# Opening of a two-block transformer kernel: modulation blocks at every second pooled tile, four of them placed behind the means

## What is computed

```python
s_c = jax.nn.silu(c)                                   # c: one vector of 1024
mod_x = s_c @ mod_w[i] + mod_b[i]                      # 1024 x 6144
sh1, sc1, g1, sh2, sc2, g2 = jnp.split(mod_x[:, None, :], N_MOD, axis=-1)
hx = x * (1.0 + sc1) + sh1
ox, oc = pool_mixer(hx, hc, pool_w[j], pool_scale[j], not last)
x = layer_norm(ALPHA * x + g1 * ox, ln_g[i, 0], ln_b[i, 0])
x = layer_norm(ALPHA * x + g2 * swiglu(x * (1.0 + sc2) + sh2, ffn_w_in[i], ffn_w_out[i]), ...)
```

## Time and profile before

| | us |
|---|---|
| median of three runs | 2856.98 |
| the three runs | 2854.58, 2856.98, 2862.43 |
| the profiled execution, its own time | 2859.71 |
| its span in the trace | 2858.0 |
| PE busy in the span | 2719.1 (95%) |
| DVE, ACT, POOL busy | 1496.9, 1031.8, 1379.0 |

### The profile page before, as it was taken

The page is one execution under the profiler, slowest core; times in us unless marked ns, Lnnn a source line. Parts: engine busy times, 40 slices in busy tenths (PEclk is TensorE's granted clock), DMA queues, the critical chain, the costliest instruction groups (busy, mean ns, idle before and its releaser), DMA issues.

```text
span 2858.0 us, 39137 instructions
## 1 busy us (share of the span) xinstructions
PE 2719.1 (95%) x14026; PEld 2175.0 (76%) x14026; DVE 1496.9 (52%) x2276; ACT 1031.8 (36%) x1792; POOL 1379.0 (48%) x895
## 2 busy tenths in 40 slices
PE   7999999999988999999997999999989999998998
PEld 2588888888766777777776888888778788886775
DVE  6665445445456555665556563645483022325666
ACT  3642222322253333333332233132442455554332
POOL 0587676676643322212221333433254477776564
PEclk9999999999999999999998999999999999998999
DMA  9211111111121101000110111111222222223333
GB/s 386 95 52 52 44 59 51 48 55 51 45 82 39 38 22 33 33 29 30 36 30 23 52 52 44 52 51 52 89 97 103 103 89 88 81 80 114 109 103 139
DMA packets 67519, 202.25 MB, mean 71 GB/s; under 512 B 17620, under 2 KB 23892, under 8 KB 65256
## 3 DMA queue, kind: packets, MB, share of 16 engines
q1 hardware_dynamic: 46624, 169.46, 17.8%
q10 hardware_dynamic: 20808, 31.61, 3.2%
HBM read 171.61 MB, written 29.44 MB: 70 GB/s over the span
## 4 chain that ended last, share of the span: by engine, by line
PE 87%; DVE 6%; ACT 2%; issue 2%; DMA 1%; POOL 1%; ACTq 0%; DVEq 0%; SPq 0%; POOLq 0%
PE ps L1046 27%; PE ps L1048 26%; PE ps L1047 26%; PE ps L1459 2%; PE ps L1114 1%; PE ps L1470 1%; DVE acc L2944 1%; PE ps L1839 1%; PE ps L1222 1%; PE ps L1189 1%; DMA mod_big<-mod_w 1%; PE ps L1200 0%; PE ps L1507 0%; PE ps L1147 0%; DVE da_al L3161 0%
## 5 line engine op out<-in xcount | busy, mean ns | idle before, releaser
L734 POOL TENSOR_TENSOR slab_hi<-slab_raw,zero 128x1024 fp32r<-128x1024 f32 x103 | 199.6, 1938 | 991.2 <-PE ps L1048 901.9
L1046 PE MATMUL ps<-h_hi,slab_hi 128*128 128x512 f32 x1616 | 645.6, 400 | 12.4 <-POOL h_lo L752 7.0
L1047 PE MATMUL ps<-h_lo,slab_hi 128*128 128x512 f32 x1616 | 634.5, 393 | 0.0
L1048 PE MATMUL ps<-h_hi,slab_lo 128*128 128x512 f32 x1616 | 633.6, 392 | 0.0
L1046 PEld LDWEIGHTS ps<-h_hi,slab_hi 128*128 128x128 f32 x1616 | 305.8, 189 | 89.0 <-issue 12.9
L1048 PEld LDWEIGHTS ps<-h_hi,slab_lo 128*128 128x128 f32 x1616 | 305.6, 189 | 66.6
L1047 PEld LDWEIGHTS ps<-h_lo,slab_hi 128*128 128x128 f32 x1616 | 306.0, 189 | 60.1
L738 POOL TENSOR_TENSOR slab_lo<-slab_raw,slab_hi 128x1024 fp32r<-128x1024 f32 x103 | 252.2, 2449 | 9.7 <-DVE mean L3044 1.7
L2970 DVE SCALAR_TENSOR_TENSOR resid<-ps,mod,resid 128x512 f32<-128x512 f32 x320 | 224.7, 751 | 0.5 <-issue 0.3
L799 POOL TENSOR_TENSOR slab_lo<-slab_raw,slab_hi 128x512 fp32r<-128x512 f32 x124 | 162.1, 1315 | 43.3 <-ACT slab_hi L2070 42.7
L1048 PE MATMUL ps<-t_hi,slab_lo 128*128 128x512 f32 x368 | 143.9, 391 | 0.0
(11 more groups left out here) (459 smaller groups left out, 5924.5 us busy)
## 6 DMA issues: line engine op xcount, KB each, us to landing
slab_raw<-w_in SPq DMA_DIRECT2D x168, 512.0 KB, 3.6
mod_big<-mod_w SPq DMA_DIRECT2D x12, 2048.0 KB, 12.1
slab_raw<-w_c SPq DMA_DIRECT2D x43, 512.0 KB, 4.1
res_scr<-resid ACTq DMA_DIRECT2D x4, 2048.0 KB, 7.2
resid<-res_scr ACTq DMA_DIRECT2D x2, 4096.0 KB, 12.4
gv_scr<-sg_t ACTq DMA_DIRECT2D x4, 2048.0 KB, 7.3
slab_raw<-gv_scr SPq DMA_DIRECT2D x16, 512.0 KB, 3.4
uz_scr<-gu_out SPq DMA_DIRECT2D x16, 512.0 KB, 3.1
```

Source lines behind the costliest of these rows:

```text
L734: pool.tensor_tensor(hi, raw[slot][:], zeros, ALU.add).then_inc(hi_done.sem, 1)
L1046: pe.matmul(dst, w_h, r_h, start=first, stop=False, skip_group_check=True)
L1047: pe.matmul(dst, w_h, r_l, start=False, stop=False, skip_group_check=True)
L1048: return pe.matmul(dst, w_l, r_h, start=False, stop=last, skip_group_check=True)
```

## The change

In the loop over pooled tiles a block and its columns stand at j = 3, 5 and 7 instead of at 2 to 6. Blocks 8 to 11 now lie behind the last means: 8 ahead of the spread of the means, 9 behind it, 10 between squares 3 and 4, 11 behind square 7 as before. ACT's copies of the rows 8, 9 and 10 move with them. SP's and POOL's lists are the same.

```diff
             for j in range(2, KT):
                 pool_tile(j)
                 pool_means(j - 2)
-                if j < 7:
-                    mod_block(j + 3)
-                if j == 4:
-                    pe.wait_ge(mod_col.sem, 4)
-                if j < 7:
-                    mod_columns(j + 2)
+                if j % 2 == 1:
+                    mod_block((j + 7) // 2)
+                    if j == 7:
+                        pe.wait_ge(mod_col.sem, 4)
+                    mod_columns((j + 5) // 2)
             pool_means(KT - 2)
             pool_means(KT - 1)
-            mod_columns(9)
+            mod_block(8)
+            mod_columns(7)
             for e in range(2):
                 spread_mean(0, e)
+            mod_block(9)
+            mod_columns(8)
+            for k in range(KT // 2):
+                square_part(0, 0, k)
             mod_block(10)
-            for k in range(KT):
+            mod_columns(9)
+            for k in range(KT // 2, KT):
                 square_part(0, 0, k)
             mod_block(11)
             spread_rstd(0, 0)
...
-            for n in range(4, 10):
+            for n in range(4, 8):
                 mod_read(n)
             act.activation(warm[:], eps[:], ACT.Sqrt)
...
             for e in range(2):
                 mean_out(0, e)
-            for n in range(5):
+            mod_read(8)
+            for n in range(2):
+                square_centred(0, n)
+            mod_read(9)
+            for n in range(2, 6):
                 square_centred(0, n)
             mod_read(10)
-            for n in range(5, KT):
+            for n in range(6, KT):
                 square_centred(0, n)
```

## The result

| us | before | changed |
|---|---|---|
| median (22 runs each) | 2861.68 | 2866.84 |
| lowest and highest | 2853.81, 2863.78 | 2858.14, 2870.17 |
| span of the profiled execution | 2858.0 | 2868.0 |

The changed kernel takes 1.0018 times as long as the one before, 95% interval 1.0012 to 1.0025: 5.2 us more, where +5.0 was forecast. The absolute forecast of 2862 stood on the median of three runs of before, 2857.0. Over 22 runs that median is 2861.7, and the changed kernel's 2866.8 lies that much higher too: as an absolute time it is 0.2 us inside the upper end of the forecast range (2855 to 2867) and where rival 3 stood. What the forecast had right is the difference.

The account below looks back on a forecast made before the run. PE was taken to bound the kernel, full from 140 to 200 us, so opening shifts reach the end. Slabs +3.0 and clock +2.0 us on the median 2857 gave 2862 us, range 2855 to 2867.

Parts of the forecast that it names:

- rival 3: Wait for square 11 passes 5.5 us, loads 10 and 11 each slow: 8.5 us slower, 2866 us or more; chance 0.14.
- Pooling loop, 4.0 us earlier: Turns 2, 4 and 6 lose block and columns, so the means are spread at 84.0 instead of 88.02 us.
- Given back behind the means, root 1 us earlier (0.3 to 4): Between means and reciprocal root an extra block and columns, up to 3.7 us, leave the root 1 us earlier.
- Slabs 10.3 us later: Slab loads queue behind loads 10 and 11, so the first slab lands at 94.0 instead of 83.70 us.
- POOL free at 102.7, sum of square 11 3.6 us later: POOL's idle 6.71 us is eaten up; square 11 starts at 102.7 instead of 99.08 us, and PE's sum waits.
- The list behind it is full, so all shifts: PE's list is full from 102.20 to 112.34 us, so everything to the last opening wait comes 3.0 us later.
- The clock, 2.0 us (0 to 4): PE's gap of 4.1 to 5 us before square 11's sum drops the clock to half, costing 2.0 us.
- Rival 1: Slabs late in the opening but the clock holds: only the 3.0 us, 2860 us; chance 0.20.
- Rival 2: Slabs load beside loads 10 and 11, so aren't late: 1 to 4 us gained, 2853 to 2856 us; chance 0.18.
- Rival 4: Clock gaps later in the kernel fall differently, 2 to 4 us each in either direction; no chance of its own given.

Follow-up runs that it names:

- e1: Changed kernel with both slab loads issued ahead of load 10 instead of behind load 11; ratio to the kernel before 0.9992 (0.9984 to 1.0001).
- e8: Changed kernel with both slab loads ahead of load 10, the same edit as e1 timed again; ratio to the kernel before 0.9991 (0.9981 to 1.0000).
- e2: Kernel before with both slab loads issued ahead of load 10; ratio to the kernel before 0.9992 (0.9983 to 1.0002).
- e3: Kernel before with its two slab loads held back until block 10 has been used; ratio to the kernel before 1.0018 (1.0009 to 1.0026).
- e4: Changed kernel with 20 matmuls without use filling PE's gap ahead of its sum of square 11; ratio to the kernel before 1.0006 (0.9997 to 1.0015).
- e7: Changed kernel, unchanged, profiled a second time; the execution took 2867.10 us.
- e9: Changed kernel with both slab loads issued between loads 10 and 11; ratio to the kernel before 1.0008 (0.9999 to 1.0018).
- e5: Kernel before, unchanged, profiled a second time; the execution took 2862.10 us.
- e6: Kernel before, unchanged, profiled a third time; the execution took 2860.27 us.

## Why the prediction was right, step by step

- **Pooling loop, 4.0 us earlier.** Right: the spread stands at 84.08, forecast 84.0, and 3.8 us earlier in the same view.
- **Given back behind the means, root 1 us earlier (0.3 to 4).** Right: the root is spread at 95.66, in before at 96.97. DVE idles 2.73 us for `mod_columns(9)`, which stand behind block 10. e1 and e8 show the net gain of this line alone: 1.3 to 1.5 us at the last wait, against a profile of before at full clock. Against e2, whose slabs are as early and whose clock fell, it is 2.9 to 3.2 us, 1.6 of them from the sum of square 11 to that of square 15 (13.74 us against 12.14 and 12.16).
- **Slabs 10.3 us later.** Right in cause, short by 0.7: load 11 and the slabs went out at 83.3 and 83.67, the first slab was used at 94.74 (forecast 94.0). e3 shows that late slabs alone make the whole loss, and e1 that without them there is none.
- **POOL free at 102.7, sum of square 11 3.6 us later.** Short by 1.0: POOL was free at 103.66 and the sum came 4.57 us later. 0.7 of it is the slab. The rest is mostly the second `slab_lo`, 2.69 us where 2.41 had been taken from a stretch in which DVE was less busy (2.94 us of the 4 from 88, against 3.71 of the 4 from 100).
- **The list behind it is full, so all shifts.** Right. Of the 4.57 us, 0.67 go in PE's own idle time (11.49 us from sum to sum at full clock, 12.16 before), so the slabs cost 3.9 us where 3.0 was forecast.
- **The clock, 2.0 us (0 to 4).** Right mechanism, term mis-sized: 3.5 and 2.5 us in the two profiles, against a run of the same list at full clock (e4), and 3.1 us in e3. The gap was 6.35 us (6.34 in e7) where 4.1 to 5 was forecast, for two reasons: the square was 1 us later, and PE had finished squares 8 to 10 at 98.4 already.
- **What the sum left out** evens this out: before, too, loses some 1.5 us of clock in the same place, in two of its three profiles, and the profile on which the sum rested had not. How often it does so in executions that were not profiled is not known. 3.9 and 3.5 make +7.4 at the opening, which is right for that one pair of profiles; +5.2 is what the medians say. Two terms too small and one left out partly cancel, so that the +5.0 fell so close to it is luck; the mechanism is not.
- **Rivals.** Rival 1 (clock holds) is refuted by the clock at 0.50. Rival 2 (slabs not late) is refuted, and e1 built it. Rival 3 came nearer in the first pair of profiles than the forecast did: the gap passed its 5.5 us, and the clock stood at 0.50 from 104 to 112 us and cost 3.5 us of its 4.0. Its sum of 8.5 is 1.1 us above that pair's 7.4, the forecast's 5.0 is 2.4 below. What did not come is its cause: load 11 landed 4.8 us behind load 10 (93.0 and 88.2), as counted. The medians' +5.2 (0.18%) are the forecast's. Block 10 and block 11 did find their loads in, by 1.7 and 0.8 us, which is why e9 could upset the second. Rival 4 (later stretches differ) is real in single executions: the time behind the last wait varies by 4.6 us between the profiles. How much of that is the clock's was not read.

e1 is faster than the changed kernel by 2.6 thousandths by its two ratios, and at or below the kernel before. Both of its intervals touch 1.000, so that it beats before is likely, not shown; e2 has the same 0.9992 with a later opening.

## What to carry to other kernels

Where one queue refills a ring of buffers, moving a consumer later moves every load behind it, those of other stages too: before a consumer is moved, follow the queue to its end, and give loads that depend on nothing a place in it where the queue stands idle. Time in hand in front of a shared engine (6.71 us here) covers such a shift only once, and what it doesn't cover becomes a gap in PE, behind which the lower clock cost another 2.5 to 3.5 us here. A transfer also decides when the engine that works on it runs beside others: in e9 slabs that came early enough for POOL fell on a chain of DVE. A sum on one profile should ask whether its baseline was a typical execution.

## What the runs showed of the hardware that I had not expected

**The clock can fall without a long gap.** In e2, e5 and e6 it fell between 100 and 108 us, behind idle gaps of at most 0.61 us that followed each other from 92.7 to 102.3. The Trainium skill, page "TensorE: Matmul & The Clock Gate", section "A second HAM failure mode: psum-queue depth-cycling", says of a kernel that cycled through PSUM banks that short idle times between groups of matmuls made the clock go up and down, unlike the single long waits of the section before; these three traces agree, as far as short idle times go. The first profile of before does not: it has the same four gaps (0.17, 0.58, 0.48 and 0.61 us) and stayed at 1.00. In e1 and e8, whose PE list is denser there (4.00 us busy of the 4 from 92 to 96, against 3.07 in before and e5), the clock stayed at 1.00. Whether the density is the reason was not separated.

The length of one gap does not settle it either. In the first trace of before, each of the 11 gaps of 2.20 to 7.05 us behind the opening was followed by half clock. Of the six gaps of 1.90 to 1.93 us between 2639 and 2786 us, three were and three were not. So the prediction's gap of 1.68 us at full clock was weaker evidence than it looked.

**DVE instructions that end with a POOL instruction.** In e9 two additions of 128x8 on DVE took 1.81 and 2.21 us; such an addition takes 0.17 us in the changed kernel while POOL idles:

```profile
93.27 0.17 DVE L2834 TENSOR_TENSOR ffn_b<-par,sc2p 128x8 f32<-128x8 f32 x1
```

They ended at 95.04 and 97.48, POOL's split instructions beside them at 95.01 and 97.45. The addition between them (L2835) began at 95.07, just ahead of POOL's next split at 95.09, and took 0.17. In the changed kernel the first `h_lo` of DVE took 2.05 us at 99.43 beside POOL's split (1.32 in e1), and POOL's second `slab_lo` beside DVE took 2.69 instead of 2.36 us. The two ends in e9 fall together; in e1, whose splits end before, the same additions take 0.17 us each. No run changed the splits alone. The Trainium skill, page "SBUF — State Buffer", section "SBUF: two separate sides", says that DVE and POOL share one pair of ports, held by whichever starts first for its whole instruction, also against a DVE instruction with two inputs in SBUF; these rows agree. It means that POOL's splits, whose time is set by a DMA, can slow a DVE chain that no semaphore ties to them: in e9 the reciprocal of the root was 3.4 us later than in e1.
